# Mixer projection units cut into quarters, unit work and turns re-placed, all copies of turned attention weights on VectorE

## What is computed

```python
x = x + 0.5 * rmsnorm(swiglu(rmsnorm(x), w_gate, w_up, w_down))     # FFN 1
u = rmsnorm(x); P = u @ w_in                                        # 1024 -> 3328 columns
q, k, v, hq, hf_fwd, hf_bwd, hi, hg = split(P)
att = rmsnorm(windowed_gqa_sink(rope(q), rope(k), v, sink))         # 8 heads of 64, |i-j| <= 128
o   = gla(sigmoid(hq), f_fwd, silu(hi)) + flip(gla(flip ...))       # 4 heads of 128, both directions
hgo = rmsnorm(o) * silu(hg)
x = x + rmsnorm(concat(att, hgo) @ w_out)
x = x + 0.5 * rmsnorm(swiglu(rmsnorm(x), ...))                      # FFN 2
```

## Time and profile before

| | before |
|---|---|
| runs (median; lowest to highest) | 1089.02 us; 1088.95 to 1090.69 |
| the profiled execution: its own time; its span | 1084.51 us; 1082.7 us |
| PE busy | 1055.2 us, 97% of the span |
| DVE, ACT, POOL busy | 423.3 (39%), 371.3 (34%), 452.8 us (42%) |
| the chain that ended last | PE 93%; DVE 3%; ACT 2%; issue 1%; DMA 1% |
| mixer and its norms (429.7 to 724 us): PE busy; granted PE clock | 282.03 of 294.30 us; 0.97 |
| the rest of the span: granted PE clock | 1.00 |

### The profile page before, as it was taken

How to read it: one execution, slowest core, us unless ns; L and a number is a source line. 1 busy time by engine, 2 the same in 40 slices (tenths; PEclk the granted TensorE clock), 3 DMA queues, 4 the chain that set the end, 5 groups by cost and what they waited for, 6 DMA issues and landing times.

```text
span 1082.7 us, 13358 instructions
## 1 busy us (share of the span) xinstructions
PE 1055.2 (97%) x5075; PEld 872.4 (81%) x5075; DVE 423.3 (39%) x605; ACT 371.3 (34%) x558; POOL 452.8 (42%) x299
## 2 busy tenths in 40 slices
PE   6999999999999999999998989999999999999997
PEld 5988888888888878888776768788888888888886
DVE  5443434343000351556554565545343434320103
ACT  6322222222122354416665465343222222221211
POOL 3444444444444158842524123035444444444440
PEclk9999999999999999999998989999999999999999
DMA  6333333333433244331111013024333333333312
GB/s 217 97 98 96 98 96 97 97 97 98 136 98 97 59 134 117 78 97 40 39 37 43 1 41 116 20 78 117 92 101 89 103 88 101 91 102 114 97 51 78
DMA packets 136300, 96.00 MB, mean 89 GB/s; under 512 B 11442, under 2 KB 120387, under 8 KB 136260
## 3 DMA queue, kind: packets, MB, share of 16 engines
q1 hardware_dynamic: 136080, 95.43, 29.3%
q10 hardware_dynamic: 180, 0.02, 0.0%
HBM read 93.34 MB, written 2.10 MB: 88 GB/s over the span
## 4 chain that ended last, share of the span: by engine, by line
PE 93%; DVE 3%; ACT 2%; issue 1%; DMA 1%; ACTq 0%; DVEq 0%
PE ps L873 19%; PE ps L874 18%; PE ps L875 18%; PE ps L880 9%; PE ps L881 9%; PE ps L882 9%; PE ps L1039 2%; PE ps L1131 2%; PE ps L1154 2%; PE ps L1073 1%; DVE YB L1326 1%; PE ps L1141 1%; ACT SQX L540 1%; PE ps L898 1%; PE ps L1050 1%
## 5 line engine op out<-in xcount | busy, mean ns | idle before, releaser
L439 POOL TENSOR_TENSOR WL<-raw,WH 128x1024 fp32r<-128x1024 f32 x132 | 317.9, 2410 | 426.2 <-ACT WH L518 426.2
L873 PE MATMUL ps<-XH,WH 128*128 128x512 f32 (+1 forms) x944 | 359.6, 381 | 0.1
L875 PE MATMUL ps<-XH,WL 128*128 128x512 f32 (+1 forms) x944 | 355.0, 376 | 0.0
L874 PE MATMUL ps<-XL,WH 128*128 128x512 f32 (+1 forms) x944 | 354.9, 376 | 0.0
L518 ACT ACTIVATE WH<-raw 128x1024 fp32r<-128x1024 f32 x162 | 171.1, 1057 | 341.5 <-PE ps L875 187.3
L873 PEld LDWEIGHTS ps<-XH,WH 128*128 128x128 f32 x944 | 178.7, 189 | 41.0 <-issue 9.5
L875 PEld LDWEIGHTS ps<-XH,WL 128*128 128x128 f32 x944 | 178.4, 189 | 32.2
L874 PEld LDWEIGHTS ps<-XL,WH 128*128 128x128 f32 x944 | 178.6, 189 | 31.5 <-issue 0.5
L456 POOL TENSOR_TENSOR WL<-raw,WH 128x256 fp32r<-128x256 f32 x120 | 95.1, 825 | 127.8 <-ACT WH L518 127.6
L880 PE MATMUL ps<-WH,hh 128*128 128x512 f32 x352 | 137.1, 390 | 0.0
L882 PE MATMUL ps<-WL,hh 128*128 128x512 f32 x352 | 137.0, 389 | 0.0
(11 more groups left out here) (164 smaller groups left out, 896.7 us busy)
## 6 DMA issues: line engine op xcount, KB each, us to landing
raw<-ffn_w_gate SPq DMA_DIRECT2D x44, 512.0 KB, 3.7
raw<-ffn_w_up SPq DMA_DIRECT2D x44, 512.0 KB, 3.7
raw<-ffn_w_down SPq DMA_DIRECT2D x44, 512.0 KB, 3.7
raw<-w_in SPq DMA_DIRECT2D x22, 512.0 KB, 3.6
raw<-w_out SPq DMA_DIRECT2D x8, 512.0 KB, 3.2
X<-x SPq DMA_DIRECT2D x4, 512.0 KB, 7.0
raw<-w_in SPq DMA_DIRECT2D x8, 256.0 KB, 3.3
out<-X SPq DMA_DIRECT2D x8, 256.0 KB, 2.0
```

The source lines that it names most:

```text
L439: pool.tensor_tensor(low, raw[:, s, :], high.bitcast(fp32), ALU.subtract).then_inc(lo_done, 1)
L873: nc.tensor.matmul(dst, WH[:, s, w], xh, start=first, stop=False)
L874: nc.tensor.matmul(dst, WH[:, s, w], xl, start=False, stop=False)
L875: return nc.tensor.matmul(dst, WL[:, s, w], xh, start=False, stop=last)
```

## The change

1. Units are cut into quarters of 6 matmuls, and the table of pieces per beat is new. Ahead of beat 0 stand two units where one stood; beats 0 to 9 take three quarters each and beat 10 two (before: 2 or 1 halves); of beats 11 to 43 all but 22 and 41 to 43 have one or two quarters (before, beats 11, 19 to 22, 30 to 33 and 40 to 43 had no unit work).
2. What follows a finished unit comes later: DVE's `copy_unit` and `out_gate` one beat after PE finishes it, `turn_unit` and `turned` two beats after.
3. `copy_even` and `copy_odd` become `copy_weights` on VectorE, first in its beat. ScalarE copies no turned weights.
4. `take_attention` stands ahead of `att_max` in its beat, its sums a beat earlier (`weights_sum`).
5. The first turns and norms of outputs (`TURN_BEAT`, `HIGH_BEAT`, `ROOT_BEAT`) come a beat later, `turn_o(1)`, `high_o(0)`, `gate_o(0)`, `low_o(0)` and `scale_o(2)` after the beats; `turn_att(2)`, `turn_att(3)` and `turn(2, 0)` come earlier among the out tiles, and `add_y(2, 3)` ahead of `split_low(2, 2)`.

The matmuls are the same in number and size; 16 copies move from ScalarE to VectorE.

```diff
-    counts = [(2, 1, 2, 1, 2, 1, 2, 1, 2, 1, 1), (0, 1, 1, 1, 1, 1, 1, 1, 0, 0, 0), (0, 1, 1, 1, 1, 1, 1, 1, 0, 0, 0),
-              (0, 1, 1, 1, 1, 1, 1, 0, 0, 0, 0)]
-    halves = [(n, p) for n in range(4 + 3, MIX_UNITS) for p in range(2)]
...
+    counts = (3,) * 10 + (2,) + (1, 1, 1, 1, 1, 2, 1, 1, 1, 1, 1) + (0, 2, 1, 2, 1, 1, 1, 1, 1, 1, 1) + (1, 2, 1, 2, 1, 2, 1, 2, 0, 0, 0)
+    parts = [(n, p) for n in range(4 + 3, MIX_UNITS) for p in range(4)]
+    return parts[:8], [[parts.pop(8) for _ in range(c)] for c in counts]
...
+        MADE = [[n for n, p in parts if p == 3] for parts in BEAT] + [[], []]
...
-        TURN_BEAT, HIGH_BEAT, ROOT_BEAT = 41, 42, 36
+        TURN_BEAT, HIGH_BEAT, ROOT_BEAT = 42, 43, 37
```

ScalarE, in a beat (`copy_odd` is gone everywhere) and behind the beats:

```diff
-                ahead(MIX + min(at + 3, MIX_UNITS + 3))
                 if g < 7:
                     mix_keys(h, g)
                 elif g >= 8:
                     copy_scores(h, g)
-                if att_item(i - 2) and i % 2:
-                    copy_odd(i - 2)
+                ahead(MIX + min(at + 3, MIX_UNITS + 3))
                 if att_item(i):
                     exp(i)
...
-            copy_odd(ITEMS - 1)
+            high_o(0)
             preload(ACT.Sqrt)
...
             high_att(2)
+            high_att(3)
             square_y(2, 0, 0)
             first_y(2, 0)
             first_x(2, 0)
-            high_att(3)
```

TensorE:

```diff
-                for k in range(KD // 2 * p, KD // 2 * (p + 1)):
+                for k in range(KD // 4 * p, KD // 4 * (p + 1)):
...
-                    pe.wait_ge(rope_done, len(TURNED))
+                    pe.wait_ge(proj_taken, len(COPIED))
+                if i < HQ:
+                    pe.wait_ge(rope_done, 2 + j)
...
             for n in range(4):
                 out_tile(1, n)
+            turn_att(2)
             out_tile(0, 6)
             out_tile(0, 7)
-            turn_att(2)
+            turn_att(3)
             for n in range(4, 8):
                 out_tile(1, n)
             for n in range(8):
-                if n == 3:
-                    turn_att(3)
+                if n == 4:
+                    turn(2, 0)
                 out_tile(2, n)
-            turn(2, 0)
```

VectorE, in a beat and behind the beats:

```diff
+                if att_item(i - 2):
+                    copy_weights(i - 2)
                 if g == 0:
                     diagonal(h)
...
-                if att_item(i - 2) and not i % 2:
-                    copy_even(i - 2)
+                if att_item(i - 3) and (i - 3) % HQ == HQ - 1:
+                    take_attention((i - 3) // HQ)
+                for n in MADE[k - 2]:
+                    if n in COPIED:
+                        turned(n)
                 if att_item(i):
                     att_max(i)
-                if att_item(i - 3) and (i - 3) % HQ == HQ - 1:
-                    take_attention((i - 3) // HQ)
+                if att_item(i - 2) and (i - 2) % HQ == HQ - 1:
+                    weights_sum((i - 2) // HQ)
+                for n in MADE[k - 1]:
+                    if n in COPIED:
+                        copy_unit(n)
+                    elif n in GATES:
+                        out_gate(n)
...
             take_y(3)
+            add_y(2, 3)
             split_low(2, 2)
-            add_y(2, 3)
             normed(2, 3)
```

More of the change, by code:

```diff
@@ L712, in out_gate_sigmoid @@
                     act.wait_ge(out_gate_ready, h)
-                if h < 2:
-                    act.wait_ge(squared, square_count("a", h))
+                else:
+                    act.wait_ge(squared, square_count("a", 1))
                 nc.scalar.activation(SQX[:, 0, :], ps[bank_of(n)][:, :], ACT.Sigmoid).then_inc(out_gate_sig, 1)
@@ L790, in _ @@
             at = 7
-            for what, n, p in FIRST:
-                if p:
+            for n, p in FIRST:
+                if p == 3:
                     at = n + 1
@@ L813, in _ @@
                     high_att(0)
[L814 to L824, removed]
+                for n in MADE[k]:
+                    at = n + 1
+                    if MIXU[n][0] == "head":
+                        head_sigmoid(n)
+                    elif MIXU[n][0] == "gate":
+                        out_gate_sigmoid(n)
+                if h and not g:
+                    take_values(h - 1)
                 if att_item(i - 4) and (i - 4) % HQ == HQ - 1:
                     square_att((i - 4) // HQ)
-            copy_odd(ITEMS - 1)
+            high_o(0)
             preload(ACT.Sqrt)
@@ L899, in turn, with quarter_unit @@
                     mm.then_inc(x_turned, 1)
-            def half(n, bank, p):
+            def quarter_unit(n, bank, p):
                 if not p:
                     pe.wait_ge(lo_done, n + 1)
-                for k in range(KD // 2 * p, KD // 2 * (p + 1)):
+                for k in range(KD // 4 * p, KD // 4 * (p + 1)):
                     mm = three(bank[:, :], n % NSLOT, k, XH[:, k, :], XL[:, k, :], not k, k == KD - 1)
-                if p:
+                if p == 3:
                     mm.then_inc(unit_used, 1)
@@ L1213, in out_tile, with part @@
                     mm.then_inc(y_ready, 1)
-            def half_unit(n, p):
+            def part(n, p):
                 if not p:
                     bank_free(n)
-                half(MIX + n, ps[bank_of(n)], p)
-            for what, n, p in FIRST:
-                half_unit(n, p)
+                quarter_unit(MIX + n, ps[bank_of(n)], p)
+            for n, p in FIRST:
+                part(n, p)
             for k in range(BEATS):
@@ L1227, in _ @@
                     att_score(i)
[L1228 to L1231, removed]
+                for n in MADE[k - 2]:
+                    if n in COPIED:
                         turn_unit(n)
-                    else:
-                        values(n)
+                for n, p in BEAT[k]:
+                    part(n, p)
+                if k and not k % 11:
+                    values(k // 11 - 1)
                 if att_item(i - 1):
@@ L1536, in copy_even, with weights_sum @@
                 w = slice(0, keys_at(i // HQ)[1] * P)
-                nc.vector.tensor_copy(PT[:, 0, w], ps[3][:, w]).then_inc(pt_even, 1)
-            def take_attention(b):
+                nc.vector.tensor_copy(PT[:, i % 2, w], ps[3][:, w]).then_inc((pt_even, pt_odd)[i % 2], 1)
+            def weights_sum(b):
                 e = b % 2
@@ L1545, in take_attention @@
                 step(nc.vector.reciprocal(r8[e], r8[e]))
+            def take_attention(b):
+                e = b % 2
                 dve.wait_ge(att_pv_done, HQ * (b + 1))
@@ L1651, in _ @@
             low_att(1)
+            weights_sum(3)
             take_attention(3)
@@ L1656, in _ @@
             low_att(2)
+            low_att(3)
             def take_y(c):
```

47 lines of the change are left out of this document (16 added, 31 removed).

## The result

| | before | changed |
|---|---|---|
| runs, median (lowest to highest) | 1089.22 us (1088.95 to 1090.69) | 1064.93 us (1064.36 to 1064.98) |
| ratio, 95% interval | | 0.9773 (0.9756 to 0.979) |
| profiled execution: own time; span | 1084.51; 1082.7 us | 1064.92; 1063.1 us |
| DVE, ACT, POOL busy | 423.3, 371.3, 452.8 us | 425.2, 363.4, 450.5 us |

The median before is over four runs here; the 1089.02 us that the prediction starts from was over three of them. The kernel is 24.3 us faster in the medians, 19.6 us in the spans of the two profiles. The forecast was 1071.0 us, 18.0 faster, and the lower end of its range was 1067.5: the direction and the mechanism held, the size did not.

A forecast was written before the change was run, and what follows sets the result against it. TensorE, 97% busy, bounds the kernel; 21.2 us of mixer idle and lost clock, less 3.2 left or new, gives 18.0 gained: 1071.0 us from the 1089.02 median, range 1067.5 to 1082.

The forecast's parts named there:

- gap A: Mixer, 584 to 600 us (beat 30): 3.46 us idle plus about 4.5 of clock, 8.0 us to win.
- B: Mixer, 632 to 642 us: 1.94 us idle plus about 3.0 of clock; 4.9 us, to go whole.
- The clock term: Mixer and its norms: mean granted clock 0.97 over 294.3 us, about 8.8 us given away.
- Tail: Out tiles: earlier turns remove a 2.44 us wait with its clock and a 1.16 us one; -5.0 us (0 to -5.0).
- Beat 30: PE wants `take_attention` at 3.6 us, VectorE's contested path takes 4.0; 0.5 us left of 8.0.
- Beats 41 to 43: Mixer beats still without unit work, VectorE's path a little longer than PE's: 0.7 us left of 2.4.
- The copies: Fifteen or sixteen copies join VectorE: 7.7 us more load there, 0.4 us cost in all (0 to 13).
- Seams: Units in 41 runs instead of 32, run ends among small fp32 matmuls: 0.5 us cost (0 to 1).
- Rival 1: One large gap survives, at another block's end or in beats without unit work: 1080 us, chance 0.20.
- rival 3: Contested multiplies let VectorE set the pace, small waits hold the clock low: slower, 1108 us, chance 0.08.
- 2 and 4: Waits only move, 1084 us, chance 0.06; change does not reach its gaps, within 2 us of 1089, 0.04.
- C: Mixer, 644 to 656 us: 2.38 us idle at clock 1.00, 2.4 us to win.

The follow-up runs named there:

- the second profile: Profile of the kernel before, run again with no edit: 1087.58 us for the profiled run.
- the fillers: Kernel before with useless matmuls added in idle TensorE gaps: 12 in beat 30, 1080.16 us; 27 in three gaps, 1077.71 us.
- the repeat: Kernel before, run again with no edit: 1088.54 us median, ratio 0.9992.

## Why the prediction was wrong

**The failed step** is the last line of the sum: the profile "stands 4.5 below the runs' median of 1089.02, to which the prediction is tied". That took the 4.5 us for something that the change leaves alone. At least 3.1 of them, by the second profile, were clock (a longer half clock behind gap A, net of a shorter one behind B), and went with the gaps. On the profile's own scale the forecast was 1066.5 and 1064.92 came: 1.6 off, of which 1.4 is that 3.2 us were left over in the sum and 1.81 in the trace. The clock term, 8.8 us, was right for the profile and mis-sized for the median execution: the fillers put it at 11.7, the profile's 8.8 with the repeat's 3.3 at 12.1. That the changed kernel's runs all agree with its profile within 0.6 us, and those of before did not, could be seen only afterwards; but runs 4.5 us above a profile with half-clock windows in it were a sign to be read, and the range should have had the offset in it as a term of its own, 0 to 4.5 us. Its lower end would then have been 1063. The direction was not luck: the waits that the prediction names are the ones that went.

Point by point, against the sum:
- *Tail*: 5.0 forecast, 5.5 measured. Right, both gaps and their cause.
- *Beat 30*: 0.5 left forecast, 0.17 measured. The multiplies took 1.01 and 1.10 us beside POOL, near the 1.12 assumed, and PE got to the values 3.85 us after the beat's start (578.17 to 582.02), not 3.6. Right.
- *Beats 41 to 43*: 0.7 left forecast; 0.19 + 0.68 measured, the latter for ScalarE. Right in size.
- *ScalarE*: 0.5 forecast, 0.66 measured at a head unit in a two-key beat. Right.
- *What is left in all*: 3.2 forecast, 1.81 idle and no half clock measured.
- *The copies* were costed at 0.4 us of PE's time and given no gain. The sum was not hurt, but the reason was incomplete: put back at their old place, they cost 9.0 us, because in short beats ScalarE comes to them too late there; alone, they cost 0.4%, because in the old order VectorE does. The forecast had neither. Their load was right (7.7 us forecast; 15.6 us for 32 copies where 16 took 7.8), but VectorE's busy time in the stage rose by 1.9 us and not by about 8, since other instructions of it took less time: the first multiply of `grow` on `GT` 742 ns against 829 in the mean, the normed x for FFN 2 749 against 1102.
- *Seams* (0.5) and the cost of `turn_att(2)` (nothing) have no run of their own.
- *Rival 1* (one large gap survives) and *rival 3* (VectorE sets the pace) did not happen, nor did 2 and 4. The argument against rival 3 called C's idle time short pieces; one of them was 1.52 us long, and at 2.00 us the same wait was followed by half clock. What the Trainium skill, "TensorE: Matmul & The Clock Gate", section "A second HAM failure mode: psum-queue depth-cycling", says of frequent micro-idles had nothing to act on here: 1.81 us of idle in the whole stage. Each single undo brought back part of rival 1, a gap with a bout behind it, in all or some of its runs (by the granted clocks: the table in half of them, VectorE's order in two of six).

The parts do not add up. Undone one by one they cost 5.5 (tail), 3.0 (table), 8.2 (gates), 5.2 (order) and 9.0 us (copies), 30.9 together where the whole is 24.3; three of them undone together cost 25.6. They all feed few gaps, and a gap costs little more than its length until the clock falls behind it: of those 25.6 us some 16 are clock. What no run undid by itself: that `copy_unit` and `turned` come later, and that the first turns and norms of outputs do. What decides how long the half clock lasts after the same gap (about 10 or 20 us behind A) was not found and stays open; in the waits and windows of the two profiles up to that point no difference was seen.

## What to carry to other kernels

An idle gap of a nearly full TensorE costs its length and then the clock that falls behind it; here the second was about half of the gain, and a useless matmul in the gap is a cheap test of which. Where a kernel's runs scatter and its profile shows half-clock windows, read the scatter as the length of these bouts and size the gain by the median run, not by the one profile. Moving work between two helper engines has no price of its own: the same 16 copies lost 0.4% in one order and were worth 0.8% in another, so place and neighbours in the queue have to be costed with it.

## What had not been expected of the hardware

- The same gap A was followed by about 10 us of half clock in one profile and by about 20 in the other. Over the span the runs had few distinct means, about 0.990, 0.987 and 0.983, with 1083, 1089 and 1091 us.
- With three gaps filled, one wait of 2.00 us in beat 40 was followed by half clock in the profile, while three of six runs had a mean clock of 0.999, so did not lose it there; in the kernel before the same wait, 1.52 us long, had left it alone. It had grown only with gap B filled.
- Adding 12 matmuls made a kernel 0.6% faster.
